# Negated scores with heads between them, the conv slots first, and post-norm, residual and pre-norm by token block

## The reference

```python
for l in range(DEPTH):                                  # DEPTH = 2
    h = rms_norm(x, pre_mix_w[l])
    u = h @ w_in[l]
    (u_conv, dq, dk, dv, gqkv, gz, b_f, b_b, a_f, a_b) = jnp.split(u, offs, axis=-1)
    y_conv = conv_module(u_conv, ...)                   # gate, 31-tap depthwise conv, layer norm, silu
    y_diff = diff_attention(dq, dk, dv, ...)            # 12 softmax maps, 6 heads, two maps to a head
    y_delta = gated_deltanet(gqkv, gz, b_f, b_b, ...)   # 3-tap short conv, then a chunked scan both ways
    y = jnp.concatenate([y_conv, y_diff, y_delta], axis=-1) @ w_out[l]
    x = x + rms_norm(y, post_mix_w[l])
    h = rms_norm(x, pre_mlp_w[l])
    y = jnp.square(jax.nn.relu(h @ w_ff1[l])) @ w_ff2[l]
    x = x + rms_norm(y, post_mlp_w[l])
```

## Time and profile before

| | |
|---|---|
| median of three runs | 3168.43 us (3165.46 to 3171.89) |
| the profiled execution | 3174.81 us |
| its span, first to last instruction | 3172.8 us |
| busy: PE, DVE, ACT, POOL | 93%, 64%, 35%, 7% |
| mean granted TensorE clock | 0.948 |
| the two layers | 0 to 514.5 us and 514.5 to 1036.5 us |

### The profile page before, as it was taken

One profiled execution on the slowest core, in us unless ns is written; L12 is line 12 of the kernel. 1 busy time (PEld: TensorE's weight loads), 2 busy tenths in 40 slices (PEclk: granted clock), 3 DMA queues, 4 the chain that ended last, 5 costly groups with the idle time before them and its releaser, 6 DMA issues.

```text
span 3172.8 us, 50021 instructions
## 1 busy us (share of the span) xinstructions
PE 2939.2 (93%) x19336; PEld 2496.4 (79%) x19340; DVE 2045.8 (64%) x3676; ACT 1096.8 (35%) x1741; POOL 227.4 (7%) x208
## 2 busy tenths in 40 slices
PE   8896999977799998989999999998898999999997
PEld 6684897867499745879899999885688989999986
DVE  1863885485388242599766666674289966666677
ACT  2321553241255230123444444441012344444443
POOL 0651000362100000000000000000000000000000
PEclk9797999977899998999999999998899999999999
DMA  5100884400388212442355555654353145445564
GB/s 208 65 17 13 321 327 148 173 15 15 145 328 302 90 50 97 169 153 79 136 183 185 185 185 185 221 199 151 133 173 131 68 174 181 182 184 184 185 239 152
DMA packets 77555, 502.31 MB, mean 158 GB/s; under 512 B 9072, under 2 KB 9456, under 8 KB 20592
## 3 DMA queue, kind: packets, MB, share of 16 engines
q1 hardware_dynamic: 71520, 481.72, 41.6%
q10 hardware_dynamic: 5904, 18.71, 1.6%
HBM read 487.82 MB, written 12.58 MB: 158 GB/s over the span
## 4 chain that ended last, share of the span: by engine, by line
PE 63%; DVE 9%; issue 1%; ACT 0%; DMA 0%; POOL 0%; DVEq 0%; ACTq 0%; POOLq 0%
PE bank L776 18%; PE bank L788 18%; PE bank L818 8%; PE bank L1814 4%; PE bank L1768 4%; PE bank L1823 4%; PE bank L1631 2%; PE bank L1651 1%; DVE sb L2039 1%; DVE sb L2032 1%; PE bank L1847 1%; DVE sb L2033 1%; DVE sb L2036 1%; DVE sb L2029 1%; DVE sb L2071 1%; DVE sb L2069 1%
## 5 line engine op out<-in xcount | busy, mean ns | idle before, releaser
L788 PE MATMUL bank<-peer_pass_high,peer_pass_hidden 128*128 128x512 f32 x1344 | 452.4, 398 | 0.0
L776 PE MATMUL bank<-peer_pass_high 128*128 128x256 f32 x1344 | 383.6, 285 | 13.8 <-DVE ring_r L863 13.8
L776 PE MATMUL bank<-peer_pass_high,ring_r 128*128 128x256 f32 x1344 | 385.8, 287 | 0.0
L776 PE MATMUL bank<-hT_r,peer_pass_high 128*128 128x256 f32 x1344 | 381.4, 284 | 0.0
L863 DVE TENSOR_TENSOR ring_r<-ring,peer_pass_high 128x1024 fp32r<-128x1024 f32 x168 | 205.8, 1225 | 194.1 <-ACT peer_pass_high L1356 194.1
L788 PEld LDWEIGHTS bank<-peer_pass_high,peer_pass_hidden 128*128 128x128 f32 x1344 | 253.9, 189 | 53.7
L776 PEld LDWEIGHTS bank<-peer_pass_high 128*128 128x128 f32 x1344 | 257.5, 192 | 22.7 <-issue 14.8
L1356 ACT ACTIVATE peer_pass_high<-ring 128x1024 fp32r<-128x1024 f32 x168 | 178.3, 1061 | 270.5 <-DMA ring<-in_experts 269.7
L788 PE MATMUL bank<-ring_r,peer_pass_hidden 128*128 128x512 f32 x672 | 267.4, 398 | 0.0
L776 PEld LDWEIGHTS bank<-hT_r,peer_pass_high 128*128 128x128 f32 x1344 | 257.9, 192 | 7.0
L776 PEld LDWEIGHTS bank<-peer_pass_high,ring_r 128*128 128x128 f32 x1344 | 257.4, 192 | 0.0
(11 more groups left out here) (345 smaller groups left out, 5890.4 us busy)
## 6 DMA issues: line engine op xcount, KB each, us to landing
ring<-in_experts SPq DMA_DIRECT2D x256, 1024.0 KB, 4.8
ring<-in_w SPq DMA_DIRECT2D x139, 1024.0 KB, 4.9
sb<-in_w_mod SPq DMA_DIRECT2D x48, 1024.0 KB, 6.8
spill<-sb ACTq DMA_DIRECT2D x22, 512.0 KB, 6.5
sb<-spill SPq DMA_DIRECT2D x44, 256.0 KB, 5.1
sb<-in_ln ACTq DMA_DIRECT2D x8, 512.0 KB, 4.8
sb<-in_post ACTq DMA_DIRECT2D x4, 512.0 KB, 4.4
sb<-in_ctx SPq DMA_DIRECT2D x2, 1024.0 KB, 17.3
```

The source lines that it names most:

```text
L776: m = pe.matmul(ps[u][:, 0:S], w, h[:, kt, :], start=(kt, i) == (0, 0), stop=(kt, i) == (KT - 1, 2))
L788: m = pe.matmul(ps[4 + 2 * tb + half][:, :], g[:, t], w, start=False, stop=False, skip_group_check=True)
```

## The change

It has four parts.

1. The slots of the conv module come first: PE projects `cg` and `ca` ahead of s0 to s4, ACT and DVE read them there, and POOL does all 31 taps in one run, ahead of the squares of the attention's output.
2. The scores are kept negated (slope times distance less product; row minimum; exponential with scale -1), so nothing is negated after the row's extreme. The heads are put between the scores: maps 0 to 3, head 0, maps 4 and 5, head 1, and so on. Map 2h is no longer scaled; the second map is added with the factor lambda * sum / sum, and the first sum's reciprocal is applied when ACT reads the head's output.
3. Post-norm, residual and pre-norm go by token block. PE ends block 0 first, squares go by halves (ACT) while DVE weights the other half, POOL needs two instructions to a root, one DVE instruction scales and adds. x is no longer scaled: PE multiplies it by a diagonal matrix of the inverse roots (two passes instead of a transpose's one).
4. The split of `hT` for the MLP is made while the banks are read: ACT writes the high part, DVE one instruction with the low part; splits of the first weights are moved into the waits of the norm.

```diff
 def layer_jobs():
-    j += [(("s", i), "act") for i in range(5)]
-    j += [("cg", "act"), ("ca", "dve"), ("gc", "dve"), ("gl", "act")]
+    j += [("cg", "act"), ("ca", "dve")] + [(("s", i), "act") for i in range(5)]
+    j += [("gc", "dve"), ("gl", "act")]
...
 def pe_transpose_x(k, pe, J, key, lay, n, rel=None):
+    banks = [J.give(pe, (key, i), lay) for i in range(4)]
+    for tb in range(TB):
+        pe.wait_ge(k.h_scaled.sem, k.h_scaled.at(n + tb + 1, lay))
+        for i in range(4):
+            for kk in range(2):
+                t = pe.matmul(k.psum[banks[i]][:, kk * S + tb * P:kk * S + (tb + 1) * P],
+                              k.x[:, tb, (2 * i + kk) * P:(2 * i + kk + 1) * P], k.diag_r[:, tb, :], start=True, stop=True)
...
 def pe_layer(k, pe, lay):
+    project(0, "cg")
+    project(1, "ca")
     for i in range(5):
-        project(i, ("s", i))
-    project(5, "cg")
-    project(6, "ca")
+        project(2 + i, ("s", i))
...
 def dve_post(k, v, st, lay, which, acc, done):
+    def weighted(tb):
+        v.wait_ge(acc.sem, acc.at(tb + 1, lay))
+        for half in (1, 0):
+            if half == 0:
+                v.wait_ge(k.y_squares.sem, k.y_squares.at(4 * which + 2 * tb + 1, lay))
+            v.tensor_tensor(k.tmp512[2 * tb + half], k.psum[4 + 2 * tb + half][:, :], half_of(k.post[which], half), ALU.mult)
+    def added(tb):
+        v.wait_ge(k.y_rstd.sem, k.y_rstd.at(2 * which + tb + 1, lay))
+        for half in range(2):
+            v.scalar_tensor_tensor(xs, k.tmp512[2 * tb + half], k.stat[:, 8 + tb:9 + tb], xs, ALU.mult, ALU.add).then_inc(done.sem, 1)
...
 def dve_layer(k, v, lay):
+    J.evac(v, "cg", lay)
+    b = J.take(v, "dve", "ca", lay)
+    v.tensor_tensor(k.cpad[:, :, PADC:PADC + S], shaped(ps[b][:, :], 2, S), k.csig[:, :, :], ALU.mult).then_inc(J.read["dve"], 1)
     J.evac(v, ("s", 4), lay)
...
-        v.scalar_tensor_tensor(k.prob[:, m_, :, :], k.dist[:, :, :], -slopes[m_ // 2], shaped(ps[b][:, :], TB, S),
-                               ALU.mult, ALU.add).then_inc(J.read["dve"], 1)
-        st.link(v.tensor_reduce(k.mx[:, m_, :], k.prob[:, m_, :, :], AX.X, ALU.max))
-        v.tensor_scalar(k.mx[:, m_, :], k.mx[:, m_, :], -1.0, None, ALU.mult).then_inc(k.sc_max.sem, 1)
+        v.scalar_tensor_tensor(k.prob[:, m_, :, :], k.dist[:, :, :], slopes[m_ // 2], shaped(ps[b][:, :], TB, S),
+                               ALU.mult, ALU.subtract).then_inc(J.read["dve"], 1)
+        v.tensor_reduce(k.mx[:, m_, :], k.prob[:, m_, :, :], AX.X, ALU.min).then_inc(k.sc_max.sem, 1)
...
-        for qb in range(TB):
-            st.done(v.tensor_scalar(k.prob[:, 2 * h, qb, :], k.prob[:, 2 * h, qb, :], k.ssum[:, 2 * h, qb:qb + 1], None, ALU.mult))
+    for m_ in range(4):
+        score(m_)
+    for h in range(DH):
+        head(h)
+        for m_ in range(2 * h + 4, min(2 * h + 6, NMAP)):
+            score(m_)
...
 def pool_layer(k, p, lay):
-    conv_taps(range(0, 20))
+    conv_taps(range(CONV_W))
     J.evac(p, ("av", DH - 1), lay)
     p.tensor_tensor(k.od2[:, :, :], k.od[:, :, :], k.od[:, :, :], ALU.mult).then_inc(k.od_sq.sem, 1)
-    conv_taps(range(20, 23))
...
-    conv_taps(range(23, CONV_W))
```

More of the change, by code:

```diff
@@ L180, in layer_jobs @@
     j += [(("d", i), "act") for i in range(1, 3)]
-    j += [(("sc", m), "dve") for m in range(NMAP)]
+    j += [(("sc", m), "dve") for m in range(6)]
     for h in range(DH + 1):
@@ L202, in layer_jobs @@
     j += [(("yx", i), "act") for i in range(2)]
-    j += [(("h2", i), "act" if i % 2 == 0 else "dve") for i in range(4)]
+    j += [(("h2", i), "dve") for i in range(4)]
     j += [("mod", "act")]
@@ L464, in slot, with pe_transpose_x @@
     return k.ring[r]
[L467 to L475, removed]
+def pe_transpose_x(k, pe, J, key, lay, n, rel=None):
+    banks = [J.give(pe, (key, i), lay) for i in range(4)]
[5 more added lines that the diff above has]
+                              k.x[:, tb, (2 * i + kk) * P:(2 * i + kk + 1) * P], k.diag_r[:, tb, :], start=True, stop=True)
+                if rel is not None:
                     rel.pay(t)
-        t.then_inc(J.filled, 1)
+            if tb == TB - 1:
+                t.then_inc(J.filled, 1)
 def pe_layer(k, pe, lay):
@@ L554, in pe_layer, with score @@
     J.evac(pe, ("d", 2), lay)
-    for m_ in range(NMAP):
+    def score(m_):
         b = J.give(pe, ("sc", m_), lay)
@@ L563, in pe_layer @@
         m.then_inc(J.filled, 1)
+    for m_ in range(6):
+        score(m_)
     def attend(h):
@@ L597, in pe_layer @@
             attend(h - 1)
+        for m_ in range(2 * h + 6, min(2 * h + 8, NMAP)):
+            score(m_)
     chunk_pairs("qk", 0)
@@ L788, in down @@
                     m = pe.matmul(ps[4 + 2 * tb + half][:, :], g[:, t], w, start=False, stop=False, skip_group_check=True)
+            if last and tb < TB - 1:
+                m.then_inc(done.sem, 1)
         m.then_inc(k.weights_used, 1)
@@ L1185, in dve_layer, with act_squares_x @@
     v.wait_ge(k.c_ready, lay + 1)
[L1186 to L1187 removed]
+    dve_experts(k, v, "ff", FF_SLOTS, k.FF, lay, None, squared=True, aside=modulation, begun=True)
+    dve_post(k, v, st, lay, 1, k.y_ff, k.x_done)
     wait(k.x_done)
     st.close("vector")
[L1193 to L1196 removed]
+def act_squares_x(k, a, lay, n, parts, done=None, at=None):
+    for i in parts:
+        tb, half = i // 2, i % 2
+        if done is not None:
+            a.wait_ge(done.sem, done.at(i + 1, at))
+        a.activation(k.junk[i], k.x[:, tb, half * 512:(half + 1) * 512], ACT.Square, scale=D ** -0.5,
+                     accum_out=k.stat[:, 6 * half + tb:6 * half + tb + 1]).then_inc(k.h_squares.sem, 1)
 def act_evac_h(k, a, J, key, col, lay):
@@ L1281, in act_layer, with exponentials, out_head @@
     a.activation(k.ekd[:, :, :], k.ekd[:, :, :], ACT.Exp).then_inc(k.gc_exp.sem, 1)
-    for m_ in range(NMAP):
-        wait(k.sc_max, m_ + 1)
-        for qb in range(TB):
-            m = a.activation(k.prob[:, m_, qb, :], k.prob[:, m_, qb, :], ACT.Exp, bias=k.mx[:, m_, qb:qb + 1],
-                             accum_out=k.ssum[:, m_, qb:qb + 1])
-            sa.done(m) if False else m.then_inc(k.sc_exp2.sem if qb == 0 else k.sc_exp.sem, 1)
-    def out_head(h):
-        copy(("av", h), k.od[:, :, h * HD:(h + 1) * HD], lambda t: shaped(t[:, 0:2 * HD], 2, HD))
+    def exponentials(maps):
+        for m_ in maps:
+            wait(k.sc_max, m_ + 1)
+            for qb in range(TB):
+                m = a.activation(k.prob[:, m_, qb, :], k.prob[:, m_, qb, :], ACT.Exp, scale=-1.0, bias=k.mx[:, m_, qb:qb + 1],
+                                 accum_out=k.ssum[:, m_, qb:qb + 1])
+                m.then_inc(k.sc_exp2.sem if qb == 0 else k.sc_exp.sem, 1)
+    def out_head(h):
+        b = J.take(a, "act", ("av", h), lay)
+        for qb in range(TB):
+            m = a.activation(k.od[:, qb, h * HD:(h + 1) * HD], ps[b][:, qb * HD:(qb + 1) * HD], ACT.Copy,
+                             scale=k.rsum[:, 2 * h, qb:qb + 1])
+        m.then_inc(J.read["act"], 1)
+    exponentials(range(6))
     for h in range(DH):
@@ L1295, in act_layer @@
             out_head(h - 1)
+        exponentials(range(2 * h + 6, min(2 * h + 8, NMAP)))
     out_head(DH - 1)
```

259 lines of the change are left out of this document (150 added, 109 removed).

## The result

The changed kernel takes **3207.5 us** (median of 4 runs, 3201.4 to 3209.8), the kernel before 3170.2 us (median of 4, 3165.5 to 3172.1): a ratio of 1.011, with a 95% interval of 1.0096 to 1.0124. It is slower, by 37.4 us where 22.7 were forecast, and the profiled executions differ by 33.7 us: 3206.5 us of span against 3172.8.

What follows compares the result with a forecast made beforehand. PE, busy 93% of the span, bounds the kernel; DVE sets attention's pace. Per layer 40.3 - 12.3 - 4.3 - 10.0 = +13.7 us; twice, less 4.7: +22.7, so 3191 us. Range 3174 to 3208; leaving out two in ten, 3158 to 3206.

Steps and rivals of the forecast that it cites:

- The sign and the mechanism: Slower: all 27 short conv instructions each wait for one POOL tap instruction, 36.2 us; first score 40.3 us late per layer.
- Rivals 1, 2 and 3: Short conv: unhindered, 3137 us, 16%; two DVE instructions per POOL instruction, 3160 us, 9%; nine products free, 3174 us, 7%.
- The chain from the short conv to the first score: Layer 0, from the short conv's end at 121.2 us to the first score at 154.8 us.
- The size: Whole kernel: +22.7 us on the profiled execution, 3191 us as median.
- The bounds of the terms: Per-term ranges: short conv 30 to 39 us, attention 8 to 14, scan 1 to 9, norm 8 to 12.
- Attention and scan: Per layer, attention gains 12.3 us with DVE setting the pace; scan gains 4.3 us with taps gone.
- Rival 4: Attention's new order waits on PE; gain falls to 3 us, 3209 us; chance 8%.
- The scan's share: Scan, free of POOL's taps: 4.3 us gained per layer, bounds 1 and 9.
- The norm term: Post-norm, residual, pre-norm between w_out and the MLP's first product: 10 us gained per layer (8 to 12).
- The start: Very start of the kernel: 0.5 us gained, between 2.5 gained and 1 lost.
- between the layers: Earlier start 2.0 us and no slow start of L495 2.2 us: 4.2 us gained, once.
- POOL's step of 1.13 us: POOL's taps: time per instruction, read from 84.95 to 86.08 us; taps to end by 131 us.

Runs made afterwards that it cites:

- one tap alone: Changed kernel with only POOL's first conv tap, the other thirty left out (output not the reference's): ratio 0.9949 to the kernel before.
- the second version with the moved split: Changed kernel with ACT's second-weight-half split moved behind its h2 bank readings and DVE's counterpart behind its own: ratio 1.0065 to the kernel before, median 3194.3 us.
- Half taps: Changed kernel with each of POOL's 62 instructions of 128x512 cut into two of 128x256: ratio 1.0015 to the kernel before.

## Why the prediction was right, and where it was short

- **The sign and the mechanism** were right. POOL's taps meet all 27 instructions of the short conv, one for one, and PE stands behind it. 34.5 us were measured for 36.2 forecast, and one tap alone shows that nothing else is in them. Rivals 1, 2 and 3 (free, two for one, nine products free) fall: the nine took 1.24 us each. The chain from the short conv to the first score was 34.3 us (119.6 to 153.9) for 33.6.
- **The size** was short. The loss of 37.4 us lies at the upper edge of the range that leaves out two in ten (3158 to 3206 us): 3206 is 37.6 above the 3168.4 us from which I reckoned, and 3207.5 itself is just past it. The bounds of the terms, added up in full, give 3162 to 3216 us and not the 3174 to 3208 stated.
- **Attention and scan** together: 16.6 forecast, 15.9 and 17.3 measured. Rival 4 (PE sets the pace) is seen only in two waits of 0.91 and 0.67 us. The scan's share alone was 2.7 and 5.8; its first 192 products took 7.47 us where the execution of the second version with the moved split had 5.82, and the granted clock from 188 to 218 us was 0.94, where the earlier trace rows have 1.00.
- **The norm term is the one that was mis-sized**: "its squares after ACT's weight split to 6.4" counted the split's own 1 us and not what it waits for. The split needs ring slot 1, and w_out's last slot is released only by PE's first product of L476 (from 333.11 us); the load is started at 333.90 us and takes 5.1 us. I had moved an instruction past others without asking when its operand arrives. 10.0 us per layer forecast, 2.9 and 3.3 measured; with the split behind the readings E + 16.0 against my E + 15.3, so the rest of the chain was right to 0.7 us. This one term, 2 x 6.9 = 13.8 us, is more than the gap between forecast (+22.7) and measured (+33.7 in the profiled executions); the short conv and its chain, 1.6 and 2.4 us under forecast, took part of it back, which is luck and not foresight.
- **The start** went 1.2 us the other way (39.53 against 38.82 us, within my bounds); between the layers 4.4 for 4.2.
- **Slips in the working.** By the prediction's own terms nine free products would save 9.6 us (36.2 - 18 x 1.34 - 2.46) and not 8.5. As before, the products and multiply-adds take 0.27 and 0.41 us, not 0.35 and 0.48. POOL's step of 1.13 us was read from its first tap alone and is 1.23 from the second on, so the taps ended at 133 us, not 131. None of these changes the outcome.
- The Trainium skill, in SBUF — State Buffer, section "SBUF: two separate sides", calls the pair of ports that VectorE and GpSimd share an exclusive lock and not a bandwidth split. Half taps against whole bear that out on DVE's side (0.72 against 1.24 us). On POOL's side the traces agree for all but some 0.35 us of DVE's instruction; see the last section.

## What to carry to other kernels

When a helper engine's work is started earlier, list what its neighbour does in the new stretch: here each of a train of short DVE instructions cost one POOL instruction, so let it lie under PE's work, spread it as its inputs arrive, or cut POOL's instructions. When an instruction is moved up in an in-order queue, price the arrival of its operand, not only its length: a 1 us copy that waited for a ring slot held a norm chain up by 6 us. And undo the parts of a bundle one by one: here part 2 (by difference) and parts 3 and 4 paid, and part 1 cost 56 us.

## What was not expected of the hardware

- **What POOL pays for the meeting.** With DVE idle its taps start 2.47 us apart (56.81, 59.28, 61.75 us), 1.04 us for a multiplication and 1.27 for an addition of the same shape, from the second tap on. Beside the nine products (0.27 us each alone) they take no longer; beside the multiply-adds (0.41 us alone) 1.10 and 1.32 us (a tap from 101.34 to 103.92 us). I had read POOL's pace under load as DVE's doing; there it is mostly its own. But longer instructions of DVE cost it more. The kernel before has POOL beside the earlier trace rows (0.55 us without POOL; first two lines) and beside two DVE instructions of 128x768 (L1029, L1030, 0.95 us in the one-tap kernel; last two):

```profile
92.71 1.24 POOL L1416 TENSOR_TENSOR sb<-sb 128x512 f32<-128x512 f32 x1
94.03 1.46 POOL L1418 TENSOR_TENSOR sb<-sb 128x512 f32<-128x512 f32 x1
...
110.98 1.63 POOL L1416 TENSOR_TENSOR sb<-sb 128x512 f32<-128x512 f32 x1
112.69 1.86 POOL L1418 TENSOR_TENSOR sb<-sb 128x512 f32<-128x512 f32 x1
```

  That is 0, 0.06, 0.20 and 0.59 us more. My estimate from these four: POOL pays DVE's length less about 0.35 us, and nothing where DVE's instruction is shorter than that. With half taps two halves take 1.42 and 1.65 us beside the multiply-adds and 1.18 and 1.41 alone, 0.12 us more each, so there it is nearer 0.3. So a short conv's meeting costs POOL almost nothing and DVE some 0.9 us an instruction. What the 0.35 us are, and why the addition is longer than the multiplication, is open.
- **Which DVE instructions wait.** Beside the taps the 4-column reciprocal took 0.17 us each time and the one of 128x1536 9.75 to 9.76 us, reductions of 128x512 0.69 us, and a two-input instruction of 128x384 with one input in a bank (L1054) 0.55 us: no wait. A two-column multiply-add took up to 1.20 us instead of 0.22 (in the kernel with part 1 undone), products of one SBUF tensor with a scalar 1.24 instead of 0.27.
